# In the first stage, key and value products follow their tiles two row chunks later instead of four, and the spill of x is issued behind the last row product

## The reference, cut to what matters

```python
shift, scale, gate = _modulation(c, mod_w, mod_b)          # silu(c) @ w + b, w is 2048 x 6144
shift_c, scale_c, gate_c = _modulation(c_ctx, mod_w, mod_b)
h = _rmsnorm(x, pre_g) * (1 + scale) + shift
hc = _rmsnorm(ctx, pre_g) * (1 + scale_c) + shift_c
proj = h @ w_in
kA_c, vA_c, kB_c, vB_c = _split_kv(hc @ w_in[:, Q_W:Q_W + KV_W])
```

## Time and profile before

| | |
|---|---|
| median of 3 runs | 2777.7 us (2777.06 to 2777.82) |
| the profiled execution | 2778.33 us, of which the traced span is 2776.5 us |
| PE busy | 2623.9 us, 95% of the span |
| DVE busy | 1687.7 us, 61% |
| ACT busy | 957.6 us, 34% |
| granted TensorE clock, mean | 0.969 of 2.4 GHz |
| the first stage (up to the first product of `gemm("hc", 1)`) | 0 to 162 us of the span |

### The profile page before, as it was taken

The page is one execution under the profiler, slowest core; times in us unless marked ns, Lnnn a source line. Parts: engine busy times, 40 slices in busy tenths (PEclk is TensorE's granted clock), DMA queues, the critical chain, the costliest instruction groups (busy, mean ns, idle before and its releaser), DMA issues. The chain is left out here.

```text
span 2776.5 us, 31689 instructions
## 1 busy us (share of the span) xinstructions
PE 2623.9 (95%) x12675; PEld 2085.1 (75%) x12675; DVE 1687.7 (61%) x2743; ACT 957.6 (34%) x1510; POOL 139.6 (5%) x117
## 2 busy tenths in 40 slices
PE   7999999999988987999998996999999999999898
PEld 5788666677766854888877883878878888888687
DVE  4455676677775668777877658665454544445432
ACT  3222344334443233323324323244443422323311
POOL 0000000000001121000110113000000000000000
PEclk8999999999999988999999997999999999999999
DMA  9935333333335544656556553532222223322332
GB/s 348 332 131 167 107 110 103 106 121 123 122 108 186 194 135 150 198 176 206 179 166 238 187 189 109 167 106 77 83 71 81 77 91 89 94 84 87 137 120 74
DMA packets 357700, 390.69 MB, mean 141 GB/s; under 512 B 11746, under 2 KB 352354, under 8 KB 354482
## 3 DMA queue, kind: packets, MB, share of 16 engines
q1 hardware_dynamic: 352144, 354.79, 40.1%
q0 software_dynamic: 5264, 33.89, 3.2%
q10 hardware_dynamic: 146, 0.00, 0.0%
HBM read 371.85 MB, written 16.78 MB: 140 GB/s over the span
## 5 line engine op out<-in xcount | busy, mean ns | idle before, releaser
L1640 PE MATMUL G<-HHI,WHI 128*128 128x512 f32 x2624 | 1112.7, 424 | 50.6 <-issue 24.5
L1640 PE MATMUL G<-HHI,WLO 128*128 128x512 f32 x2624 | 1032.9, 394 | 0.0
L1640 PE MATMUL G<-HLO,WHI 128*128 128x512 f32 x2624 | 1030.4, 393 | 0.0
L1237 DVE TENSOR_TENSOR WLO<-RAW,WHI 128x1024 fp32r<-128x1024 f32 x376 | 458.8, 1222 | 315.3 <-ACT WHI L947 312.3
L1640 PEld LDWEIGHTS G<-HHI,WHI 128*128 128x128 f32 x2624 | 498.0, 190 | 182.3 <-issue 65.5
L947 ACT ACTIVATE WHI<-RAW 128x1024 fp32r<-128x1024 f32 x376 | 394.9, 1053 | 622.4 <-PE G L1640 583.2
L1640 PEld LDWEIGHTS G<-HLO,WHI 128*128 128x128 f32 x2624 | 499.0, 190 | 113.2 <-issue 19.1
L1640 PEld LDWEIGHTS G<-HHI,WLO 128*128 128x128 f32 x2624 | 496.3, 189 | 109.8
L1243 DVE SCALAR_TENSOR_TENSOR MACC<-MRAW,SC,MACC 128x256 f32<-128x256 f32 x840 | 437.3, 521 | 94.6 <-DMA MRAW<-in_od_mod_w 34.2
L1640 PE MATMUL G<-WHI,HHI 128*128 128x256 f32 x640 | 186.8, 292 | 0.0
L1640 PE MATMUL G<-WLO,HHI 128*128 128x256 f32 x640 | 181.2, 283 | 0.0
(11 more groups left out here) (241 smaller groups left out, 2389.4 us busy)
## 6 DMA issues: line engine op xcount, KB each, us to landing
RAW<-in_w_in SPq DMA_DIRECT2D x128, 512.0 KB, 3.8
MRAW<-in_od_mod_w SPq DMA_DIRECT2D x96, 512.0 KB, 4.8
MRAW<-in_w_ada SPq DMA_DIRECT2D x96, 512.0 KB, 4.9
RAW<-in_ev_w_in SPq DMA_DIRECT2D x80, 512.0 KB, 3.9
RAW<-in_od_w_in SPq DMA_DIRECT2D x64, 512.0 KB, 4.1
MRAW<-in_ev_mod_w SPq DMA_DIRECT2D x54, 512.0 KB, 5.1
RAW<-in_ev_w_out SPq DMA_DIRECT2D x32, 512.0 KB, 3.5
RAW<-in_od_w_out SPq DMA_DIRECT2D x32, 512.0 KB, 3.5
```

The costliest lines, as they stand in the source:

```text
L1237: return e.o.tensor_tensor(o, a, b, op)
L1640: return e.o.matmul(o, l, r, start=start, stop=stop, skip_group_check=True)
```

## The change

The pieces of pair m enter `ready` in the same iteration in which `h_pair` m is issued, behind that iteration's own pieces, instead of one row later; so the first is issued at chunk 8m + 11 instead of 8m + 13. All four quarters of the spill stand behind the last row product (`p_row` 63).

```diff
-            ready, near = [], []
+            ready = []
...
                 if c == 1 and n > 0:
                     put("row_cols", n - 1)
-                    ready += near
-                    near = []
                     if n % 2 == 0:
                         put("h_pair", n // 2 - 1)
-                        near = pieces(n // 2 - 1)
-                if i > 51 and i % 4 == 3:
-                    put("x_spill", i // 4 - 13, i)
                 for _ in range((0, 2, 0, 3)[i % 4]):
                     if ready:
                         kv_piece(*ready.pop(0))
+                if c == 1 and n > 0 and n % 2 == 0:
+                    ready += pieces(n // 2 - 1)
             put("row_cols", len(order0) - 1)
             put("h_pair", 7)
-            put("x_spill", 3, 63)
-            for piece in ready + near + pieces(7):
+            for q in range(4):
+                put("x_spill", q, 63)
+            for piece in ready + pieces(7):
                 kv_piece(*piece)
```

## The result

| | before | changed |
|---|---|---|
| median | 2777.4 us (4 runs, 2776.76 to 2777.82) | 2792.0 us (4 runs, 2789.08 to 2793.13) |
| ratio, 95% interval | | 1.0051 [1.0034, 1.0069] |
| profiled execution, its span | 2778.33, 2776.5 us | 2793.13, 2791.4 us |
| granted TensorE clock, mean | 0.969 | 0.966 |
| cols(3), cols(15), next product behind the stage | 57.68, 146.53, 162.14 us | 59.42, 160.58, 177.74 us |

A forecast was written before the change was run, and what follows sets the result against it. PE was taken to bound the kernel, busy 95% of the span. The terms 12.9 + 1.6 - 4.9 + 0 + 0 + 6.0 = +15.6 us on 2778.33 gave 2793.9, forecast 2793 us as the median; range 2784 to about 2804.

The forecast's parts named there:

- Six new waits: Pairs 1 to 6: the tile needs 5.18 us, work ahead fills 3.03, so PE waits 2.15 us each, +12.9 us.
- The beginning: Start of the first stage: reordered pieces of pair 0 bring cols(3) at 59.3 us instead of 57.68, +1.6 us.
- The spill behind the last row: Between cols(3) and cols(15): PE's waits for late row chunks 59, 61 and 63 go, -4.9 us.
- The spill's own end: Behind the last row product: the four quarters take 11 to 12 us, hidden by pair 7's products, 0.
- Behind cols(15): End of the stage: the gap grows to about 3.1 us, but tile 14's product begins 5.07 us behind in both, 0.
- The clock: Behind the new gaps: the TensorE clock falls to its low level four more times at 1.5 us each, +6.0 us.
- the price list: PE's times at full clock: cols 0.47 us, two key pieces 2.27, two row chunks 1.00, a value piece 0.78.
- no clock falls: Rival: the six waits come but the clock holds, +9.6 us, 2787 us; chance 0.25.
- Loads set the stage: Rival: loads outlast PE's 16.3 us period, hiding the new waits; -4.9 us, 2773; chance 0.07, shared with tiles ready early.
- many and longer falls: Rival: six or seven clock falls at up to 3 us, up to +21 us, 2798 to 2808 us; chance 0.13.

The follow-up runs named there:

- e1: The kernel before with only the late spill, all four quarters behind the last row product: 2771.56 us, ratio 0.9987.
- e7: e1 with k_copy issued right behind the last key piece, ahead of pair 7's last value pieces: 2768.5 us, ratio 0.9968 to the kernel before.
- e2: The changed kernel with the spill issued early again, so only the order of the products is changed: 2793.8 us, ratio 1.0064 to the kernel before.
- e10: The program of e2 run again, beside e9: 2792.01 us, ratio 1.006 to the kernel before.
- e4: The changed kernel with four needless products ahead of each of the six products that wait for a tile: 2785.57 us, ratio 1.0039 to the kernel before.
- e9: The changed kernel itself, measured again: 2791.7 us, ratio 1.006 to the kernel before.
- e3: The changed kernel with three value pieces instead of two between the cols and the new tile: 2785.28 us, ratio 1.0035 to the kernel before.
- e5: The changed kernel with DVE and ACT finishing a pair's first tile before going on with the second: 2776.92 us, ratio 0.9998 to the kernel before.
- e6: The changed kernel with the edits of both e5 and e3: 2775.57 us, ratio 0.9992 to the kernel before.
- e8: e3 with the weight split that follows a pair's last key piece issued behind h_pair: 2783.47 us, ratio 1.002 to the kernel before.

## Why the prediction was right, step by step

1. *Six new waits*, 12.9: measured 12.33, 2.03 to 2.07 us each instead of 2.15. The tile took 5.18 us as read (59.42 to 64.60). The work ahead of it was 3.14, not 3.03.
2. *The beginning*, 1.6: measured 1.74. The sum put every operation behind the two key pieces at full clock, without saying why the clock should rise earlier than before. It did: from 52 to 54 us its mean is 1.00 in the changed kernel and 0.60 before. From cols(1) on the beginning costs 2.05 us, as PE was 0.3 us ahead there by chance.
3. *The spill behind the last row*, -4.9: no wait for a load is left from 53 us on, so the size holds as the difference to the profiled execution of before. In the old order the late spill by itself does this: the stretch is 4.25 us shorter in e1 and 4.97 in e7, though the median of e1 shows only 3.5. In the new order part of it, or nearly all, would have gone without the late spill (waits of 0.32 us left in e2, about 2.1 us and a fall in e10). The step counted all of it as the spill's doing, where the slower PE does some.
4. *The spill's own end*, 0: right. The forecast had 11 to 12 us for the four quarters and 6 us of slack. In the changed kernel they take at most 12.5 us, and ACT comes to KTA 19.0 us behind the first issue (158.05 to 177.02), 1.55 of it the fall behind cols(15): 6.5 us of slack, 5 without the fall. In e7, where the copy does wait for them, it starts 14.3 us behind the first issue (140.88 to 155.18), so the time of the spill varies and the slack can shrink to about 4 us.
5. *Behind cols(15)*, 0 without the clock: the gap is 3.05 us as forecast, and the tile is there 5.07 us behind the cols as before.
6. *The clock*, four more falls at 1.5 us, 6.0: measured three more (three in the six gaps, one behind cols(15), less the one at 162 us) at 1.55 to 1.56, 4.7 us. The mechanism is confirmed by e4; the number was one too high, and no row of the forecast gave it: it was a guess between none and seven. The kernel with no falls is not what the chip did: of the 26 gaps of 2.03 to 2.07 us in all traces 15 had the low level behind them. The Trainium skill's page "TensorE: Matmul & The Clock Gate", section "Why this matters for your kernels", warns only of idle gaps of more than about 3 us; these gaps are shorter, so on them the measurement decides against it. The gap of 3.05 us behind cols(15) lies at that limit, so the page's rule did not make the term plainly 0, as the forecast has it.

Put together as in the forecast: 12.33 + 1.74 - 4.89 + 0.19 (work slightly longer than the price list has it) + 4 falls (6.23) less the one of before (1.55) = 14.05 us, and 14.9 is what the span shows. The 0.85 us between them are of the size of the fall behind the gap that ends at 307.14 us (0.97), which the forecast did not count. The forecast of 15.6 was thus near for the right reasons, with two terms sized 0.6 and 1.3 us too high. That it came within 1 us is partly luck: the same kernel was 16.9 us above before in e9, and single executions of the kernel before lie between 2771.25 and 2780.33 us.

The rivals: "no clock falls" is out in every trace of this order (three or four falls in the stretch of the six gaps). "Loads set the stage" is out (no such wait, rate 273 to 296 GB/s); "many and longer falls" is out in this trace (clock 1.00 again within 5 us of three gaps; a fall costs 1.56 us).

## What to carry to other kernels

When a consumer is moved closer to its producer, compare two lengths from the trace: from the product that releases the chain to the first product that uses its result, and the work that stands between them in the new order; what is missing is a wait per round. Where it is missing, shorten the chain first (finish the tile that is needed first, keep unrelated splits off its engine), since waits of about 2 us also cost clock here, in more than half of the cases. Here it also paid to put a bulk transfer that nobody needs soon behind the last urgent load (e1), and the step that overwrites its source where other work covers the wait (e7).

## What the runs showed of the hardware

The clock's answer to gaps is not a matter of their length alone. Of 22 gaps of 0.26 to 1.32 us (e3, e5, e6, e8) none had the low level behind it; of 26 gaps of 2.03 to 2.07 us (the changed kernel, e2, e3, e9, e10) 15 had, in the changed kernel every second one, in e2 and e3 in another order; of two gaps of 2.32 and 2.33 us behind cols(15) one had (e8, 0.66) and one had not (e3, 1.00); all five of 3.04 or 3.05 us had. Here are two of the stretches, of the gap of 2.32 us in e3 and that of 2.33 us in e8:

```profile
161.00:166.00 5.00, 5.00 (x33) 4.51 (x32) 0.00 (x0) 0.78 (x1) 0.00 (x0) 1.00 0.83 342
```

```profile
156.00:161.00 5.00, 4.68 (x18) 4.00 (x19) 0.57 (x2) 0.00 (x0) 0.00 (x0) 0.66 0.96 395
```

One gap of 1.99 us (e5, behind cols(15)) had none. Three places show it best, since the work around them is the same in every kernel. Behind PE's wait for KTA at the end of the stage, 1.78 us long in each of eleven traces, the clock fell in three (before, e2, e4). Behind a gap of 2.25 to 2.30 us between 285 and 312 us it fell in six of twelve. Behind the next gap, 1.75 to 2.07 us, it fell in one of twelve (before). What decides between gaps of equal length the runs don't tell. It does make equal programs differ by one or two falls of 1.56 us each (the order of e2 and e10 had four falls in six gaps in one trace and three in five in the other), and single executions of one kernel spread by several us (e5: 2771.02 to 2782.1).
